# Branch mixture with the branch outermost, and seven of its column pairs by block products

## The chip, the cores and the metric

One core of a Trainium2 chip runs the whole program in one launch. The metric is device microseconds of one execution. The times before the change are 2878.73, 2878.84 and 2879.1 us; the median is 2878.84 us.

## The reference, cut to what matters

Four layers run on a sequence of 512 rows with 1024 columns in float32: two hybrid layers, then a pooling layer and an attention layer. The change is in the two hybrid layers, at the end of their first half:

```python
branches = jnp.stack([ret, gla_o, fox_o], axis=2).astype(h.dtype)
y_br = jnp.einsum('bsnw,nwd->bsnd', branches, w_br)
gates = jax.nn.sigmoid(h @ w_mg + b_mg).reshape(b, s, N_BRANCH, D_MODEL)
mixed = jnp.sum(gates * y_br, axis=2) @ w_o
x = x + (gate1[:, None, :] * mixed).astype(x.dtype)
h2 = modulate(rms_norm(x, norm2_g), shift2, scale2)
u, g = jnp.split(h2 @ w_up, 2, axis=-1)
```

Three branches of 512 columns each are projected to 1024 columns, weighted by three gates of 1024 columns that come from the normed input `h`, summed, and projected by `w_o`. A feed-forward part with 2816 columns (22 tiles of 128) follows.

## The kernel before

**Products.** Every float32 factor is kept as a high part (fp32r) and a low remainder, and a product is three matmuls: high by high, high by low, low by high (`dot`, L490 to L504; the matmuls are L496 to L498). A *tile* is 128 output columns by 512 rows: eight input blocks by three matmuls, 24 matmuls of 512 columns, summed in one PSUM bank (`tile_of`, L509). A weight *chunk* (128 by 1024 numbers, 512 KB) is loaded by SyncE's queue into one of six slots (L3391); ScalarE writes its high part (L1503, four chunks ahead) and GpSimd its low part in place of the raw numbers (L3376). A slot is loaded again once TensorE has done with its chunk.

**Banks.** `take_bank` (L484) hands out PSUM banks in turn from the list that is in force, and one running count serves all lists: `b = self.order[self.turn % len(self.order)]`. The lists are BIG3 (b0, b1, b2), BIG4 (b0, b1, b2, o) and BIG6 (b0, b1, b2, o, s0, s1). The count is set to 0 at the end of the prologue (L737) and at the start of the attention layer (L1324), and nowhere between. TensorE waits, before the first matmul into a bank, for the event that `free` holds for it: the instruction that last read the bank's previous contents. A *take* is one such call.

**Order of the work in a hybrid layer** (`schedule`, L400): retention, forgetting attention, gated linear attention, `gated` (eight tiles), the mixture, `w_o`, the feed-forward part `ffn`, `w_down`. Each engine has its own written-out program in the same order and runs it strictly in that order; semaphores tie them together. In the first hybrid layer, the chunks of `ada` (modulation weights, worked on by VectorE at L2526, with a short folding product at L782 that takes a bank) are stepped beside the mixture and later work.

**The mixture** (`mixing`: TensorE L1099, ScalarE L1916, VectorE L2815). A *unit* is one branch and one pair of output tiles `d` = 2dp, 2dp+1. TensorE makes two gate tiles (`mg`, 24 matmuls each) and two branch tiles (`br`, four blocks by three, 12 matmuls each) and takes four banks. ScalarE puts the sigmoid of a gate tile in SG (L1927); VectorE multiplies the branch tile with it (L2829 or L2832) and adds to the sum MX (L2834). After the third branch, ScalarE writes the high part MH (L1934) and VectorE the low part ML (L2838) of the finished tile. The 12 units of a layer run with dp outside and the branches 0, 2, 1 inside; MX has room for two tiles. Two units run beside `gla_attention`, under BIG3; then come the four tiles of `gated(l, 1)` under BIG3, and ten units under BIG4. `w_o` (`out_proj`, L1137) starts with three output tiles at once, block by block (L1164 to L1166), so that it takes three banks within its first nine matmuls. It stays under BIG4.

**The feed-forward part** (`ffn`: TensorE L1197, ScalarE L2052, VectorE L3018). Tiles `up` and `gateup` alternate, f = 0 to 21. The first four f (HEAD, eight takes) stand under BIG4, then BIG6 holds to the end of `ffn`, and `w_down` is under BIG4 again. The bank of `up` f is free when VectorE's second convolution step has read it (`conv`, L2895; a layer of the first two has `up_freed` = `conv`); that of `gateup` f when VectorE has multiplied it (L2903). For some f (`PAIRS_OF`) the two tiles are made together by `pair` (L1232) in the manner of Strassen and Winograd: seven half products of 4 blocks by 3 matmuls of 256 columns (84 matmuls, L1226 to L1228), in place of 48 matmuls of 512 columns; it takes three banks in place of two. Its operands are sums: of quarters of the input (TR, TH, TL: once per layer, `halves_whole` L2919, `halves_sums` L2927, `halves_low` L2939 on VectorE, `halves_high` L2007 on ScalarE), and of quarters of the two weight chunks (ER, EH, EL and one chunk slot: `pair_sums` L2947, `pair_low` L2965, `pair_high` L2014). The parts of the result that two quarters share go through MP (`pair_copies` L2030, `pair_out` L2984). The sums of the input are made by VectorE during f = 1 to 3, between the convolutions.

Of the kernel before, what the change touches and what calls it, by code (L numbers as in the profile page):

```python
# [64 lines left out]
def pair_block(i, f):  # L65

    return PAIRS_OF[i].index(f) % 2
# [187 lines left out]
class Kernel:  # L255
# [26 lines left out]
    def block(self, i, f):  # L282

        b = pair_block(i, f)
        return tuple(self.t[x][:, b, :, :] for x in ("EH", "EL", "ER"))
# [17 lines left out]
def ffn_norm(i):  # L303
    return (1, 3, 5, 7)[i]
# [160 lines left out]
class TensorSteps(Steps):  # L465
# [633 lines left out]
    def mixing(self, l, dp, branches):  # L1099
# [6 lines left out]
        for n in branches:  # L1106
            for u in range(2):
                d = 2 * dp + u
                key = ("mg", l, d, n)
                yield from self.project(wmg, n * 1024 + d * 128, key, lambda key=key: m.atake.at(*key))  # L1110
# [26 lines left out]
    def out_proj(self, name, i, norm):  # L1137
# [6 lines left out]
        place = (lambda k: (LAST + k) % ROOM) if name in ("w_down", "ffn_w_down") else (lambda k: k)  # L1144
# [52 lines left out]
    def ffn(self, i):  # L1197
# [10 lines left out]
        for f in range(HEAD, KF):  # L1208
            if f not in PAIRS_OF[i]:
                for key, ap, c0, freed in jobs(f):  # L1210
                    for _ in self.project(ap, c0, key, freed):
                        yield BUSY if f == KF - 1 else None
            else:
                yield from self.pair(i, f, up_freed)
            if f in DOWN:
                yield from self.down(i, wd, *DOWN[f])
# [15 lines left out]
    def pair(self, i, f, up_freed):  # L1232

        m, t, K = self.m, self.t, self.K
        wu, cu, wg, cg, _ = ffn_weights(self.I, i)
        na = self.weight(wu, 0, 8, cu + f * 128, 128)
        nb = self.weight(wg, 0, 8, cg + f * 128, 128)
# [9 lines left out]
        T1, T3, T2, T4 = [(t["TH"][:, j, :, :], t["TL"][:, j, :, :]) for j in range(4)]  # L1247
        left, right = slice(0, 256), slice(256, 512)

        def H(j, c):  # L1250
            return t["HH"][:, 4 * j:4 * j + 4, c], t["HL"][:, 4 * j:4 * j + 4, c]

        bc_, ba, bd = [self.take_bank((x, i, f)) for x in ("up", "mid", "gateup")]
# [9 lines left out]
                          [("up", i, f)])  # L1263
        yield BUSY
        self.half_product(G[:, left], A22, T4, True, [m.vtake.at("t", i, 3), m.atake.at("mid5", i, f)],
                          [("gateup", i, f), ("chunk", na), ("chunk", nb)])
        yield BUSY
        self.free[ba] = m.vtake.at("mid", i, f)
        self.free[bc_] = up_freed(f)
        self.free[bd] = m.vtake.at("gateup", i, f)  # L1270
# [215 lines left out]
class ScalarSteps(Steps):  # L1486
# [429 lines left out]
    def mixing(self, l, dp, branches):  # L1916
        e, q, m, t = self.e, self.q, self.m, self.t
        c = pcol(l, "b_mg")
        for n in branches:
            for u in range(2):  # L1920
                d = 2 * dp + u
                key = ("mg", l, d, n)
                yield from self.tile()
                j = c + 8 * n + d
                before = ("mixed", l, d, (None, 2, 0)[n]) if n else ("mixed", l, d - 2, 1)
                q.wait_ge(m.dense.at(*key), m.vtake.at(*before) if n or dp else None)
                e.activation(t["SG"][:, u, :], self.bank[self.K.where.get(key, "b0")][:, :], ACT.Sigmoid,  # L1927
                             bias=t["PAR"][:, j:j + 1]).then_inc(*m.atake.up(key))
            self.chunk()
            yield None  # L1930
            yield None
        for d in (2 * dp, 2 * dp + 1) if n == 1 else ():
            q.wait_ge(m.vtake.at("mixed", l, d, 1))
            e.activation(t["MH"][:, d, :], t["MX"][:, d % 2, :], ACT.Copy).then_inc(*m.atake.up(("mh", l, d)))  # L1934
# [95 lines left out]
    def pair_copies(self, i, f, late):  # L2030

        e, q, m, t, K = self.e, self.q, self.m, self.t, self.K
        A, G = [self.bank[K.where.get((x, i, f), "b0")] for x in ("mid", "gateup")]
# [3 lines left out]
        e.activation(t["MP"][:, 0:3:2, :], A[:, :].rearrange("p (h c) -> p h c", h=2), ACT.Copy,  # L2037
# [4 lines left out]
        e.activation(t["MP"][:, 1, :], G[:, 256:512], ACT.Copy).then_inc(*m.atake.up(("mid5", i, f)))  # L2042
# [240 lines left out]
class VectorSteps(Steps):  # L2283
# [531 lines left out]
    def mixing(self, l, dp, branches):  # L2815
        e, q, m, t = self.e, self.q, self.m, self.t
        SG, MX = t["SG"], t["MX"]
        for n in branches:
            for u in range(2):
                yield from self.tile()  # L2820
            self.next_chunk()
            for u in range(2):
                d = 2 * dp + u
                yield None
                out = self.out_of(("br", l, d, n))
                q.wait_ge(m.dense.at("br", l, d, n), m.atake.at("mg", l, d, n))
                if n == 0:
                    q.wait_ge(m.vtake.at("mix", l, d - 2) if dp else None)
                    e.tensor_tensor(MX[:, u, :], out[:, :], SG[:, u, :], ALU.mult).then_inc(  # L2829
                        *m.vtake.up(("br", l, d, 0), ("mixed", l, d, 0)))  # L2830
                else:
                    e.tensor_tensor(SG[:, u, :], out[:, :], SG[:, u, :], ALU.mult).then_inc(*m.vtake.up(("br", l, d, n)))  # L2832
                    q.wait_ge(m.vtake.at("br", l, d, n))
                    e.tensor_tensor(MX[:, u, :], MX[:, u, :], SG[:, u, :], ALU.add).then_inc(  # L2834
                        *m.vtake.up(("mixed", l, d, n)))
# [83 lines left out]
    def halves_whole(self, i):  # L2919

        e, q, m, t = self.e, self.q, self.m, self.t
        for j, (k, c) in enumerate(((0, 0), (0, 256), (4, 256), (4, 0))):
            q.wait_ge(m.vnorm.at("h", ffn_norm(i), 1, 7))
            e.tensor_tensor(t["TR"][:, j, :, :], t["HH"][:, k:k + 4, c:c + 256].bitcast(F32),
                            t["HL"][:, k:k + 4, c:c + 256].bitcast(F32), ALU.add).then_inc(*m.vtake.up(("whole", i, j)))

    def halves_sums(self, i):  # L2927

        e, q, m, TR = self.e, self.q, self.m, self.t["TR"]
        q.wait_ge(m.vtake.at("whole", i, 1))  # L2930
        e.tensor_tensor(TR[:, 0, :, :], TR[:, 1, :, :], TR[:, 0, :, :], ALU.subtract).then_inc(*m.vtake.up(("traw", i, 0)))
        q.wait_ge(m.vtake.at("whole", i, 2), m.vtake.at("traw", i, 0))
        e.tensor_tensor(TR[:, 1, :, :], TR[:, 2, :, :], TR[:, 1, :, :], ALU.subtract).then_inc(*m.vtake.up(("traw", i, 1)))
        q.wait_ge(m.vtake.at("traw", i, 1))
        e.tensor_tensor(TR[:, 2, :, :], TR[:, 0, :, :], TR[:, 2, :, :], ALU.subtract).then_inc(*m.vtake.up(("traw", i, 2)))
        q.wait_ge(m.vtake.at("whole", i, 3), m.vtake.at("traw", i, 2))
        e.tensor_tensor(TR[:, 3, :, :], TR[:, 3, :, :], TR[:, 2, :, :], ALU.add).then_inc(*m.vtake.up(("traw", i, 3)))

    def halves_low(self, i, js):  # L2939

        e, q, m, t = self.e, self.q, self.m, self.t
        for j in js:
            q.wait_ge(m.atake.at("t", i, j))
            e.tensor_tensor(t["TL"][:, j, :, :], t["TR"][:, j, :, :], t["TH"][:, j, :, :].bitcast(F32),
                            ALU.subtract).then_inc(*m.vtake.up(("t", i, j)))

    def pair_sums(self, i, f):  # L2947
# [8 lines left out]
        before = pair_before(i, f, 2)  # L2956
# [27 lines left out]
    def pair_out(self, i, f, row):  # L2984

        e, q, m, t = self.e, self.q, self.m, self.t
        A, MP = self.out_of(("mid", i, f)), t["MP"]
        if row == 0:
            q.wait_ge(m.dense.at("up", i, f), m.atake.at("mid", i, f), m.atake.at("mid5", i, f))
# [4 lines left out]
            C = self.out_of(("up", i, f))[:, :].rearrange("p (h c) -> p h c", h=2)  # L2994
            e.tensor_tensor(C, C, MP[:, 0:2, :], ALU.subtract).then_inc(*m.vtake.up(("out1", i, f)))
        else:
            q.wait_ge(m.dense.at("gateup", i, f), m.vtake.at("mid", i, f))
            G = self.out_of(("gateup", i, f))[:, :].rearrange("p (h c) -> p h c", h=2)
# [454 lines left out]
def places(nc):  # L3453
    with ExitStack() as ctx:
# [199 lines left out]
```

## Time and profile before

| | us |
|---|---|
| median of three runs | 2878.84 |
| the profiled execution | 2875.43 |
| its span, first to last instruction | 2873.6 |
| TensorE busy | 2838.0 (99% of the span) |
| VectorE busy | 1606.0 (56%) |
| ScalarE busy | 1176.6 (41%) |
| GpSimd busy | 1123.3 (39%) |
| mean granted TensorE clock (share of 2.4 GHz) | 0.998 |

The profiled execution is 1.8 us longer than its span. It is one execution; the three timed runs lie within 0.4 us of each other and their median is 3.4 us above it. Times in the rows are counted from the first instruction. Matmuls are pipelined: the duration of one in a row is longer than the distance to the start of the next, and that distance is what a stream of matmuls costs.

### The profile page before, as it was taken

What the parts mean: (1) busy time and instruction counts of PE and PEld (TensorE: products, weight loads), DVE (VectorE), ACT (ScalarE), POOL (GpSimd) and SP (SyncE); (2) the same over time, 40 slices, a digit from 0 to 9 for tenths busy, and PEclk for the clock granted to TensorE, in tenths of its full rate; (3) what the DMA queues carried; (4) which work ended last, traced back from release to release, by engine and by line L of the source; (5) the groups of instructions that cost most, each with busy time, mean ns of one, the idle gap of its engine ahead of it and who ended that gap; (6) DMA issues with size and microseconds to landing.
All of it is one profiled execution on the core that took longest, in us unless ns stands there. A gap on an engine that the chain in (4) does not pass through costs nothing.

```text
span 2873.6 us, 37367 instructions
## 1 busy us (share of the span) xinstructions
PE 2838.0 (99%) x15599; PEld 2397.8 (83%) x15599; DVE 1606.0 (56%) x2244; ACT 1176.6 (41%) x1797; POOL 1123.3 (39%) x461
## 2 busy tenths in 40 slices
PE   8999999999999999999999999999999999999999
PEld 5777888888888877788898988888999877789998
DVE  6444572367675624422266755648668456676683
ACT  4336333342333424532344434444334466443433
POOL 2332345334445332344435344543334423333432
PEclk9999999999999999999999999999999999999999
DMA  8331353346564422233333333333333322233332
GB/s 259 104 103 52 100 194 117 95 141 202 195 200 127 113 80 59 74 96 96 88 101 92 97 107 89 103 96 92 100 110 103 104 67 67 75 93 98 109 103 76
DMA packets 507292, 314.25 MB, mean 109 GB/s; under 512 B 14290, under 2 KB 478836, under 8 KB 506868
## 3 DMA queue, kind: packets, MB, share of 16 engines
q1 hardware_dynamic: 507124, 311.87, 37.0%
q8 instruction: 123, 2.02, 0.3%
q14 instruction: 45, 0.37, 0.0%
HBM read 309.73 MB, written 2.10 MB: 109 GB/s over the span
## 4 chain that ended last, share of the span: by engine, by line
PE 93%; DVE 3%; ACT 1%; DMA 1%; SPq 1%; issue 0%; POOL 0%; DVEq 0%; ACTq 0%
PE b L496 16%; PE b L498 16%; PE b L497 16%; PE o L496 4%; PE o L498 4%; PE o L497 4%; PE s L498 3%; PE s L496 3%; PE s L497 3%; PE b L1226 2%; PE b L1228 2%; PE b L1227 2%; PE s L1226 1%; PE s L1228 1%; PE s L1227 1%; PE b L1164 1%
## 5 line engine op out<-in xcount | busy, mean ns | idle before, releaser
L3376 POOL TENSOR_TENSOR lo<-raw,hi 128x1024 fp32r<-128x1024 f32 (+2 forms) x451 | 1121.0, 2496 | 1721.1 <-ACT hi L1503 1371.8
L1503 ACT ACTIVATE hi<-raw 128x1024 fp32r<-128x1024 f32 (+2 forms) x454 | 464.5, 1035 | 318.7 <-DMA raw<-in_w_up_dram 92.9
L496 PE MATMUL b<-HH,hi 128*128 128x512 f32 x1296 | 517.7, 399 | 0.0
L498 PE MATMUL b<-HH,lo 128*128 128x512 f32 x1296 | 505.2, 390 | 0.0
L497 PE MATMUL b<-HL,hi 128*128 128x512 f32 x1296 | 505.1, 390 | 0.0
L496 PEld LDWEIGHTS b<-HH,hi 128*128 128x128 f32 x1296 | 243.3, 188 | 57.9 <-issue 7.1
L498 PEld LDWEIGHTS b<-HH,lo 128*128 128x128 f32 x1296 | 243.3, 188 | 51.9
L497 PEld LDWEIGHTS b<-HL,hi 128*128 128x128 f32 x1296 | 243.5, 188 | 50.2 <-issue 1.4
L2526 DVE SCALAR_TENSOR_TENSOR AA<-raw,CA,AA 128x512 f32<-128x512 f32 x140 | 143.5, 1025 | 3.5
L496 PE MATMUL b<-FH,hi 128*128 128x512 f32 (+1 forms) x385 | 141.7, 368 | 0.9 <-POOL lo L3376 0.9
L497 PE MATMUL b<-FL,hi 128*128 128x512 f32 (+1 forms) x385 | 141.3, 367 | 0.0
L498 PE MATMUL b<-FH,lo 128*128 128x512 f32 (+1 forms) x385 | 141.3, 367 | 0.0
L2909 DVE TENSOR_TENSOR FL<-CB,FH 128x512 fp32r<-128x512 f32 x88 | 82.6, 938 | 62.2 <-ACT FH L1997 62.2
L2021 ACT ACTIVATE EH<-ER 128x1024 fp32r<-128x1024 f32 x38 | 40.3, 1062 | 179.3 <-DVE ER L2958 179.3
L1997 ACT ACTIVATE FH<-CB 128x512 fp32r<-128x512 f32 x88 | 55.6, 632 | 126.6 <-DVE CB L2903 125.6
L1990 ACT ACTIVATE CB<-CB 128x512 f32<-128x512 f32 x88 | 55.4, 630 | 121.6 <-DVE CB L2895 72.0
L2832 DVE TENSOR_TENSOR SG<-b,SG 128x512 f32<-128x512 f32 x21 | 14.5, 691 | 155.6 <-PE b L498 155.6
L496 PE MATMUL o<-HH,hi 128*128 128x512 f32 x248 | 96.5, 389 | 0.0
L497 PE MATMUL o<-HL,hi 128*128 128x512 f32 x248 | 96.5, 389 | 0.0
L498 PE MATMUL o<-HH,lo 128*128 128x512 f32 x248 | 96.5, 389 | 0.0
L1927 ACT ACTIVATE SG<-b,PAR 128x512 f32<-128x512 f32 x43 | 29.6, 689 | 155.3 <-PE b L498 155.3
L2977 DVE TENSOR_TENSOR lo<-raw,hi 128x1024 fp32r<-128x1024 f32 x38 | 90.0, 2369 | 0.0
(654 smaller groups left out, 6837.9 us busy)
## 6 DMA issues: line engine op xcount, KB each, us to landing
raw<-in_w_up_dram SPq DMA_DIRECT2D x88, 512.0 KB, 4.1
raw<-in_w_ada_dram SPq DMA_DIRECT2D x80, 512.0 KB, 4.9
raw<-in_w_in_dram SPq DMA_DIRECT2D x76, 512.0 KB, 4.1
raw<-in_w_mg_dram SPq DMA_DIRECT2D x48, 512.0 KB, 3.8
raw<-in_ffn_w_gate_dram SPq DMA_DIRECT2D x44, 512.0 KB, 3.9
raw<-in_ffn_w_up_dram SPq DMA_DIRECT2D x44, 512.0 KB, 3.9
raw<-in_w_down_dram SPq DMA_DIRECT2D x32, 448.0 KB, 3.8
raw<-in_ffn_w_down_dram SPq DMA_DIRECT2D x32, 448.0 KB, 3.9
```

The costliest lines, as they stand in the source:

```text
L496: e.matmul(out, wh, xh, start=start and k == 0, stop=False)
L497: e.matmul(out, wh, xl, start=False, stop=False)
L498: mm = e.matmul(out, wl, xh, start=False, stop=stop and k == last)
L1226: e.matmul(out, wh[:, c], xh[:, k, :], start=start and k == 0, stop=False, skip_group_check=True)
L1227: e.matmul(out, wh[:, c], xl[:, k, :], start=False, stop=False, skip_group_check=True)
L1228: mm = e.matmul(out, wl[:, c], xh[:, k, :], start=False, stop=k == 3, skip_group_check=True)
L1503: e.activation(t["hi"][:, c % NSLOT, 0:w], K.raw[:, c % NSLOT, 0:w], ACT.Copy).then_inc(*m.hi.up(c))
L1997: e.activation(t["FH"][:, f % ROOM, :], t["CB"][:, f % 2, :], ACT.Copy).then_inc(*m.atake.up(("fh", i, f)))
L2526: a = e.scalar_tensor_tensor(out=AA[:, :], in0=raw[:, k * 512:k * 512 + 512], scalar=CA[:, kk:kk + 1], in1=AA[:, :], op0=ALU.mult, op1=ALU ...
L2909: e.tensor_tensor(t["FL"][:, f % ROOM, :], t["CB"][:, f % 2, :], t["FH"][:, f % ROOM, :].bitcast(F32), ALU.subtract).then_inc(*m.vtake.up( ...
L2977: e.tensor_tensor(t["lo"][:, s, :], K.raw[:, s, :], t["hi"][:, s, :].bitcast(F32), ALU.subtract).then_inc(*m.vtake.up(("lo", na + 1 if K.p ...
L3376: e.tensor_tensor(t["lo"][:, s, 0:w], K.raw[:, s, 0:w], t["hi"][:, s, 0:w].bitcast(F32), ALU.subtract).then_inc(*m.lo.up(n))
```

## The change

The mixture is turned around in both layers: the branch is the outer loop (0, 2, 1) and dp the inner one, as units f = 0 to 11. The sum MX has eight tiles and stays raw until the third branch; MH and ML are then written in the last four units, ML in place of MX. Units 2 to 11 run under BIG6 in place of BIG4. In the second hybrid layer alone, units 5 to 11 make their two gate tiles by `pair`, with one buffer of weight sums in place of two, and with the pair's shared parts (mMP) in the place of SG. The sums of the input for it are made in units 2 to 4. `ffn` and the rest keep their lists and their code; `out_proj` reads MH and ML at shifted places. The core of the diff:

```diff
-            (5, 6, 7, 8, 9, 10, 12, 13, 14, 15, 16, 17, 19, 20))
+            (5, 6, 7, 8, 9, 10, 12, 13, 14, 15, 16, 17, 19, 20),
+            (), (5, 6, 7, 8, 9, 10, 11))
+MIX_BRANCHES = (0, 2, 1)
...
-    return PAIRS_OF[i].index(f) % 2
+    return PAIRS_OF[i].index(f) % 2 if i < 4 else 0
...
-        fill = chain(P.gated(l, 0), P.mixing(l, 0, (0, 2)))
+        fill = chain(P.gated(l, 0), P.mixing(l, (0, 1)))
         weave(P.gla_attention(l), fill)
         drain(beside(P.gated(l, 1), ada, 8))
+        P.order = BIG6
+        drain(beside(P.mixing(l, range(2, 12)), ada, 28))
         P.order = BIG4
-        drain(beside(chain(P.mixing(l, 0, (1,)), *[P.mixing(l, dp, (0, 2, 1)) for dp in (1, 2, 3)]), ada, 28))
...
+        for f in units:
+            n, dp = MIX_BRANCHES[f // 4], f % 4
+            keys = [("mg", l, 2 * dp + u, n) for u in range(2)]
+            if f in PAIRS_OF[4 + l]:
+                c0 = n * 1024 + dp * 256
+                yield from self.pair(4 + l, f, (wmg, c0), (wmg, c0 + 128), m.atake.at(*keys[0]), m.atake.at(*keys[1]))
...
-        bc_, ba, bd = [self.take_bank((x, i, f)) for x in ("up", "mid", "gateup")]
+        bc_, ba, bd = [self.take_bank(key) for key in (up, ("mid", i, f), gate)]
...
+                q.wait_ge(m.vtake.at("out%d" % (u + 1), i, f) if pair else m.dense.at(*key),
+                          m.vtake.at("mixed", l, 2 * ((f - 1) % 4) + u, MIX_BRANCHES[(f - 1) // 4]) if f else None)
...
+            if f == 3 and PAIRS_OF[i]:
+                self.halves_high(i, (0, 1, 2))
+            if f == 4 and PAIRS_OF[i]:
+                q.wait_ge(m.dense.at("br", l, 7, 0))
+                self.halves_high(i, (3,))
...
+        if i >= 4:
+            q.wait_ge(m.vtake.at("mixed", i - 4, 2 * ((f - 1) % 4) + 1, MIX_BRANCHES[(f - 1) // 4]))
...
+            if f == 2 and PAIRS_OF[i]:
+                self.halves_whole(i)
+            if f == 3 and PAIRS_OF[i]:
+                self.halves_sums(i)
...
+            if f in PAIRS_OF[i]:
+                self.next_chunk()
+                self.next_chunk()
+                yield BUSY
+                yield BUSY
+                if g is not None:
+                    self.pair_sums(i, g)
+                yield BUSY
+                self.pair_out(i, f, 0)
+                yield BUSY
+                self.pair_out(i, f, 1)
+                if g is not None:
+                    self.pair_low(i, g, 0)
...
+            self.next_chunk()
+            yield None
+            branch(0)
+            if g is not None:
+                self.pair_low(i, g, 1)
+            yield None
+            branch(1)
+            if g is not None:
+                self.pair_low(i, g, 2)
...
-        before = pair_before(i, f, 2)
+        before = pair_before(i, f, 2 if i < 4 else 1)
         q.wait_ge(m.dense.at("block", i, before) if before is not None else None)
...
-        area("MH", 36, [128, 8, S], F32R)
+        area("MH", 28, [128, 8, S], F32R)
         area("ML", 20, [128, 8, S], F32R)
+        area("MX", 20, [128, 8, S])
         area("SG", 8, [128, 2, S])
-        area("MX", 10, [128, 2, S])
+        area("mMP", 8, [128, 3, 256])
```

Here g is the next unit where that one is made by `pair`, and `branch(u)` is the multiplication and the addition of one branch tile.

## Rows read from the trace of the kernel before

**Rows 1.** The page: busy time, share of the span and instructions by engine.

```profile
PE 2838.0 (99%) x15599; PEld 2397.8 (83%) x15599; DVE 1606.0 (56%) x2244; ACT 1176.6 (41%) x1797; POOL 1123.3 (39%) x461
```

**Rows 2.** Windows, both mixtures: length, busy per engine, clock, DMA share, GB/s.

```profile
300.00:545.00 245.00, 245.00 (x1192) 201.87 (x1191) 114.49 (x133) 82.20 (x99) 104.80 (x43) 1.00 0.42 130
1250.00:1425.60 175.60, 175.60 (x776) 145.46 (x775) 37.13 (x44) 54.13 (x66) 78.35 (x33) 1.00 0.33 96
```

**Rows 3.** Timeline of TensorE in layer 2's mixture: two matmuls, 36 apart.

```profile
1384.81 0.39 PE L496 MATMUL b<-HH,hi 128*128 128x512 f32 x1
...
1392.97 0.39 PE L496 MATMUL b<-HH,hi 128*128 128x512 f32 x1
```

**Rows 4.** Timeline of TensorE: a pair's first matmul, the first after its 84.

```profile
2697.94 0.28 PE L1226 MATMUL s<-HH,hi 128*128 128x256 f32 x1
...
2708.02 0.40 PE L496 MATMUL b<-FH,hi 128*128 128x512 f32 x1
```

**Rows 5.** By source line: the pair's work on VectorE; ns shortest/median/longest.

```profile
L2958 DVE TENSOR_TENSOR ER<-raw x38: 1212/1216/1220, 1542.0 to 2789.8; 128x1024 f32<-128x1024 f32 x38
L2981 DVE TENSOR_TENSOR EL<-ER,EH x38: 677/683/2891, 1549.3 to 2797.1; 128x512 fp32r<-128x512 f32 x38
L2977 DVE TENSOR_TENSOR lo<-raw,hi x38: 1209/2338/3444, 1546.0 to 2793.8; 128x1024 fp32r<-128x1024 f32 x38
L2995 DVE TENSOR_TENSOR b<-b,MP x19: 698/699/700, 1617.2 to 2806.9; 128x512 f32<-128x512 f32 x19
L2834 DVE TENSOR_TENSOR MX<-MX,SG x32: 692/1212/1999, 338.4 to 1426.5; 128x512 f32<-128x512 f32 x32
```

**Rows 6.** Timeline of VectorE at the head of layer 2's feed-forward part.

```profile
1495.64 9.03 DVE L2924 TENSOR_TENSOR TR<-HH,HL 128x1024 f32<-128x1024 f32 x4
...
1515.83 2.55 DVE L2944 TENSOR_TENSOR TL<-TR,TH 128x1024 fp32r<-128x1024 f32 x2
...
1521.12 4.55 DVE L2944 TENSOR_TENSOR TL<-TR,TH 128x1024 fp32r<-128x1024 f32 x2
1525.59 0.74 DVE L2892 SCALAR_TENSOR_TENSOR CB<-b,PAR,CB 128x511 f32<-128x511 f32 x1
1526.36 0.75 DVE L2895 SCALAR_TENSOR_TENSOR CB<-b,PAR,CB 128x510 f32<-128x510 f32 x1
1527.87 0.69 DVE L2903 TENSOR_TENSOR CB<-CB,b 128x512 f32<-128x512 f32 x1 [0.77 <-PE b L498]
```

**Rows 7.** Timeline of TensorE there: the first matmul of `up` 4.

```profile
1516.77 0.39 PE L496 MATMUL s<-HH,hi 128*128 128x512 f32 x1
```

**Rows 8.** Timeline of ScalarE there: the activation after the convolution of f = 3.

```profile
1527.14 0.63 ACT L1990 ACTIVATE CB<-CB 128x512 f32<-128x512 f32 x1 [5.89 <-DVE CB L2895]
```

**Rows 9.** Windows at the kernel's start; the granted clock is the third number from the end.

```profile
15.00:20.00 5.00, 2.03 (x10) 2.03 (x10) 3.85 (x6) 4.41 (x7) 0.00 (x0) 0.66 1.13 327
20.00:25.00 5.00, 5.00 (x24) 2.21 (x23) 2.73 (x4) 1.21 (x2) 0.00 (x0) 0.50 1.10 348
25.00:30.00 5.00, 4.12 (x30) 1.29 (x28) 3.58 (x7) 1.38 (x2) 0.00 (x0) 0.82 1.10 348
```

**Rows 10.** Timeline of TensorE there: after an idle stretch, and twice the same work.

```profile
17.97 0.59 PE L722 MATMUL t<-ones,SS 128*128 128x1 f32 x2 [3.45 <-DVE SS L2375]
...
21.48 4.13 PE L697 MATMUL s<-ada,CA 128*32 128x512 f32 x16
...
35.42 2.34 PE L697 MATMUL s<-ada,CA 128*32 128x512 f32 x16
```

**Rows 11.** Timelines: the last tile ahead of `w_o`, and of `w_down`, and their readers.

```profile
1425.61 0.39 PE L1164 MATMUL b<-MH,hi 128*128 128x512 f32 x1
...
1425.81 0.69 DVE L2832 TENSOR_TENSOR SG<-o,SG 128x512 f32<-128x512 f32 x1 [0.78 <-PE o L498]
...
1782.97 0.39 PE L1164 MATMUL b<-FH,hi 128*128 128x512 f32 x1
...
1783.17 0.69 DVE L2903 TENSOR_TENSOR CB<-CB,b 128x512 f32<-128x512 f32 x1 [3.09 <-PE b L498]
```

More of the change, by code:

```diff
@@ L303, in ffn_norm @@
 def ffn_norm(i):
-    return (1, 3, 5, 7)[i]
+    return (1, 3, 5, 7, 0, 2)[i]
 def norm_weights(t, nid):
@@ L1143, in out_proj @@
         halves = WHOLE[nid]
-        place = (lambda k: (LAST + k) % ROOM) if name in ("w_down", "ffn_w_down") else (lambda k: k)
+        place = ((lambda k: (LAST + k) % ROOM) if name in ("w_down", "ffn_w_down") else
+                 (lambda k: (k + 4) % 8) if name == "w_o" else (lambda k: k))
         def entries(d):
@@ L1213, in ffn @@
             else:
-                yield from self.pair(i, f, up_freed)
+                yield from self.pair(i, f, (wu, cu + f * 128), (wg, cg + f * 128), up_freed(f), m.vtake.at("gateup", i, f))
             if f in DOWN:
@@ L1230, in half_product, with pair @@
             mm.then_inc(*m.dense.up(*keys))
-    def pair(self, i, f, up_freed):
+    def pair(self, i, f, above, below, up_freed, gate_freed):
         m, t, K = self.m, self.t, self.K
-        wu, cu, wg, cg, _ = ffn_weights(self.I, i)
-        na = self.weight(wu, 0, 8, cu + f * 128, 128)
-        nb = self.weight(wg, 0, 8, cg + f * 128, 128)
+        up, gate = pair_keys(i, f)
+        na = self.weight(above[0], 0, 8, above[1], 128)
+        nb = self.weight(below[0], 0, 8, below[1], 128)
         assert nb == na + 1
@@ L2032, in pair_copies @@
         e, q, m, t, K = self.e, self.q, self.m, self.t, self.K
-        A, G = [self.bank[K.where.get((x, i, f), "b0")] for x in ("mid", "gateup")]
+        A, G = [self.bank[K.where.get(key, "b0")] for key in (("mid", i, f), pair_keys(i, f)[1])]
+        MP = t["MP" if i < 4 else "mMP"]
         g = pair_before(i, f, 1)
@@ L2813, in gated, with mixing, branch @@
                 *m.vtake.up(("gated", l, which, h)))
-    def mixing(self, l, dp, branches):
+    def mixing(self, l, units):
         e, q, m, t = self.e, self.q, self.m, self.t
         SG, MX = t["SG"], t["MX"]
[L2818 to L2822, printed above, removed]
+        i = 4 + l
+        for f in units:
+            n, dp = MIX_BRANCHES[f // 4], f % 4
+            g = f + 1 if f + 1 in PAIRS_OF[i] else None
+            def branch(u):
                 d = 2 * dp + u
-                yield None
+                p = (d + 4) % 8
                 out = self.out_of(("br", l, d, n))
@@ new lines, in mixing @@
+            if f == 3 and PAIRS_OF[i]:
+                self.halves_sums(i)
+            if f == 4 and PAIRS_OF[i]:
+                q.wait_ge(m.dense.at("br", l, 7, 0))
+            if f in PAIRS_OF[i]:
+                self.next_chunk()
+                self.next_chunk()
+                yield BUSY
+                yield BUSY
+                if g is not None:
+                    self.pair_sums(i, g)
+                yield BUSY
+                self.pair_out(i, f, 0)
+                yield BUSY
+                self.pair_out(i, f, 1)
+                if g is not None:
+                    self.pair_low(i, g, 0)
+            else:
+                if g is not None:
+                    self.pair_sums(i, g)
+                for _ in self.tile():
+                    yield BUSY if f == 4 else None
+                if g is not None:
+                    self.pair_low(i, g, 0)
+                for _ in self.tile():
+                    yield BUSY if f == 4 else None
+                if f == 3 and PAIRS_OF[i]:
+                    self.halves_low(i, (0, 1, 2))
+                if f == 4 and PAIRS_OF[i]:
+                    self.halves_low(i, (3,))
@@ new lines, in mixing @@
+            self.next_chunk()
+            yield None
+            branch(0)
+            if g is not None:
+                self.pair_low(i, g, 1)
+            yield None
+            branch(1)
+            if g is not None:
+                self.pair_low(i, g, 2)
+            for d in (2 * dp, 2 * dp + 1) if n == 1 else ():
+                q.wait_ge(m.atake.at("mh", l, d))
+                p = (d + 4) % 8
+                e.tensor_tensor(t["ML"][:, p, :], MX[:, p, :], t["MH"][:, p, :].bitcast(F32), ALU.subtract).then_inc(
+                    *m.vtake.up(("mix", l, d)))
@@ L2986, in pair_out @@
         e, q, m, t = self.e, self.q, self.m, self.t
-        A, MP = self.out_of(("mid", i, f)), t["MP"]
+        up, gate = pair_keys(i, f)
+        A, MP = self.out_of(("mid", i, f)), t["MP" if i < 4 else "mMP"]
         if row == 0:
-            q.wait_ge(m.dense.at("up", i, f), m.atake.at("mid", i, f), m.atake.at("mid5", i, f))
+            q.wait_ge(m.dense.at(*up), m.atake.at("mid", i, f), m.atake.at("mid5", i, f))
             e.tensor_tensor(MP[:, 1:3, :], MP[:, 1:3, :],
```

123 lines of the change are left out of this document (77 added, 46 removed).

## The prediction

> **What bounds the kernel now.** I read the page first: TensorE is busy for 99% of the span [rows 1], so only what TensorE issues, and the time in which it issues nothing, can count. Then the windows over the two mixtures: TensorE is busy in every microsecond of both, at full clock, while VectorE works 37 of 176 us in layer 2's and 114 of 245 us in layer 1's [rows 2]. There is no stall in the mixture to be removed. A gain can only come from fewer or shorter matmuls, and a loss from a wait that the new order puts in front of TensorE. Then the timelines for the price of a matmul, and last, because the change alters how many banks are taken, the places where the list of banks changes.
>
> **What is removed and added on TensorE.** In a stream, 36 matmuls of 512 columns take 1392.97 - 1384.81 = 8.16 us, 0.2267 us each [rows 3]; the 84 matmuls of a pair take 2708.02 - 2697.94 = 10.08 us, 0.120 us each [rows 4]. Two gate tiles cost 48 x 0.2267 = 10.88 us, a pair 10.08 us: 0.80 us less. Seven pairs in one layer: **-5.60 us**. The branch tiles stay, so a pair unit lasts 10.08 + 24 x 0.2267 = 15.52 us. The Trainium skill (TensorE: Matmul & The Clock Gate, Back-to-back issue gap) prices a warm matmul at N / 2.4 GHz plus 2.5 ns, about 109 ns at 256 columns and 216 ns at 512; by that the pairs would give 8.3 us. The rows say 120 and 227 ns, and I take the rows.
>
> **Can the pairs be fed?** The buffer of weight sums is single now, so VectorE starts the next unit's sums only when five of the seven half products are done: 60 x 0.120 + 0.28 = 7.5 us after the pair's start. From there, in VectorE's order: sums of 1024, 512 and 512 numbers, 1.22 + 0.69 + 0.69, done at 10.2; three combining steps of 0.7, 12.2; the low part of the first sums, as wide as L2958, 1.22; branch tile 0 (a multiplication of 0.69 and an addition of 0.69 to 2.0); a low part of 1.2 to 3.4; branch tile 1, for whose product it must wait to 15.7; the last low part, 0.68 [rows 5]. The long ends are those of operations that meet a low part on GpSimd: L2977 lasts 3.44 at most against 1.21, so 2.2 are lost to one such meeting [rows 5]. GpSimd makes two low parts per unit; with one meeting of 0.4 and one of 2.0 the chain ends at about 20.5. TensorE wants the last one for the fifth half product of the next pair, at 15.52 + 5.76 = 21.3. So it holds with 0.8 us to spare: cost **0**, upper end 1 us in each of six pairs. ScalarE's new wait for the previous unit's sum before it writes mMP (it lies over SG) ends at 19.8; TensorE needs that copy at 22.7. Behind it stand only the highs of the unit after. GpSimd's and SyncE's queues keep three chunks per unit in the same order; two slots now come free together, at 10.1 us, and the next use is 15 us on. The sums of the input (12 operations of 1.2 us, up to 3.4) fall into units 2 to 4, where VectorE was idle for four fifths of the time [rows 2]; they delay ScalarE's highs by some 7 us, and those run four chunks, some 20 us, ahead. The reordered sums, MH, ML and the folds are the same operations at other times; they cost nothing while VectorE has that room, and if it had not, branch banks would come free late, which six banks allow for 10 us.
>
> **The bank count.** This is where I expect the time to go. The count is never reset in the hybrid layers, so I count takes from the zero at L737. Layer 1 up to `w_o`: 8 + 4 + 16 + 6 + 4 + 8 + 4 + 40 and two folds = 92, before and after. The rest of layer 1 (11 + 60 + 11, four folds) gives 178; layer 2 up to `w_o` gives 268 before. Now each pair takes one bank more: 275. `w_o` takes 11, so `ffn` begins at 279 before and 286 after. Before, `up` 4 is take 287, and 287 mod 6 = 5 is s1: the row of `up` 4 indeed shows an s bank [rows 7]. After, `up` 3 is take 292, under BIG4 that is b0; `up` 4 is take 294, under BIG6 also **b0**. The bank that came round after several takes comes round after two.
>
> `up` 4 must therefore wait for the convolution of f = 3. VectorE ends that at 1526.36 + 0.75 = 1527.11 [rows 6], because the sums of the input stand in front of it: 9.03 us for the first four, then ScalarE's part, then 2.55 and 4.55 us for the low parts [rows 6]. None of that waits for `up` 4. TensorE could start `up` 4 at 1516.77 [rows 7]. A semaphore passes to ScalarE in 0.03 us [rows 8]; with 0.2 us for TensorE to pick up weights and start, the wait is 1527.11 - 1516.77 + 0.2 = **+10.5 us**. Behind it on TensorE stands everything; ScalarE and VectorE catch up meanwhile. `gateup` 4 then sits in gate 3's bank, read at 1527.87 + 0.69, long before TensorE gets there. Bounds: if the second group of low parts went as quickly as the first, 2.55 in place of 4.55, the wait is 8.5 us; if the first group were as slow as the second, 12.5.
>
> **The clock after the wait.** At the start of the kernel TensorE was idle for 3.45 us [rows 10], and the granted clock averages 0.66 in that window, 0.50 in the next, 0.82 in the third [rows 9]: it fell to 1.2 GHz at about 16.6 us, still idle, and rose to 2.4 GHz at about 26.8 us, 5.3 us after the dense work at 21.48 began. The same 16 matmuls took 4.13 us at the lower level and 2.34 at the higher [rows 10]. An idle time of 10.5 us should do the same. 5.3 us of work at 2.34/4.13 of the speed gives away 5.3 x (1 - 0.567) = **+2.3 us**; bounds 0 and 4.
>
> **Two small waits of the same kind.** Under BIG6 the last two branch tiles of layer 1 are takes 90 and 91, b0 and b1; `w_o`'s first three are 92 to 94 under BIG4: b0, b1, b2. The second wants the last branch tile's bank 3 x 0.2267 = 0.68 us after `w_o`'s start. Before, that tile's reader starts 0.20 us after `w_o`'s first matmul and lasts 0.69 [rows 11]: free at 0.89, a wait of some 0.2, with the restart **+0.4 us** (0 to 1). Layer 2's `w_o` gets o, b0, b1, whose readers are long done. At the end of layer 2's `ffn` (62 takes under BIG6: ten pairs, eight plain f, 16 for `down`) the count is 356 in place of 349: `w_down` starts on b0, b1, b2 and the last `gateup` tile is take 355, b1. Its reader also starts at 0.20 and lasts 0.69 [rows 11]: **+0.4 us**. From there lists of four follow lists of four until the third layer's head, which gets a distance of four; the attention layer sets the count to zero.
>
> **The sum.** -5.6 + 10.5 + 2.3 + 0.4 + 0.4 = +8.0 us. Against the profiled execution's own 2875.43 us that is 2883.4. That execution is 3.4 us under the median of the timed runs, so as a median I predict 2878.84 + 8.0 = **2886.8 us**. The case's own range is 2882 to 2891: the wait's bounds (2 either way) and the clock's, not all at once.
>
> **The rivals.**
> 1. *No wait at `up` 4.* If the bank is not the same one, or its reader is done by then, what is left is -5.6 + 0.4 + 0.4 = -4.8: **2874.0 us**, not slower. For it: the old kernel starts `up` 4 without a stall. Against: the count reproduces the s bank before, and VectorE's 1527.11 does not depend on TensorE. It decides if VectorE's convolution of f = 3 ends by 1516.8, 10.3 us earlier than now.
> 2. *A shorter wait and no fall of the clock.* 8.5 us and 0: -5.6 + 8.5 + 0.8 = +3.7, **2882.5 us**, inside 0.2%. For it: the second low parts were slowed by GpSimd, which may stand otherwise. Against: ScalarE's and GpSimd's order there is untouched.
> 3. *The pairs stall too.* Single buffer, VectorE in its long durations at every step: six more pairs at 1 us and the forecast's terms: +14, **2892.8 us**. For it: 3.44 and 2.89 us stand in the rows for low parts [rows 5]. Against: a unit has only two GpSimd operations to run into.
> 4. *The pairs gain by the formula.* 8.3 us in place of 5.6 by a matmul stream that runs at the pure column rate: +5.3, 2884.1 us. Every pair in the trace runs at 0.120. That is the rule of the skill's page above.
>
> **How the numbers follow.** Chances: the forecast 0.72, rival 1 0.11, rival 2 0.09, rival 3 0.07, rival 4 0.01. 0.2% of the time is 5.8 us, about what a measurement of this kernel can tell from no change. The forecast lies over it, as does rival 3: slower 0.80 with a little of rival 2's upper end. Rival 1 at -4.8 lies within it, unless its small terms vanish and something more is won: 0.03 faster, 0.08 same. With rivals 2 and 4 the same is 0.17. The range must leave out no more than 0.2: it takes in the forecast's own, rival 2, part of rival 3, and the 3 us by which single executions differ: 2878 to 2892.
>
> **What would show it.** In the changed trace: pairs in layer 2's mixture of 84 starts 0.120 us apart and no gap between units; at the head of layer 2's `ffn` one idle stretch of TensorE of some 10 us ahead of `up` 4, ended by VectorE's L2895, `up` 4 in a b bank, and a clock of 0.50 for some 5 us behind it; gaps under 0.5 us in `w_o` of layer 1 and `w_down` of layer 2. No such stretch there makes the prediction wrong at its main step; gaps ahead of the fifth half product would speak for rival 3.

## The result and the profile after

The changed kernel takes 2887.69 us (median of 7 runs, 2884.65 to 2888.86), the kernel before, measured again beside it, 2877.94 (median of six): a ratio of **1.0034**, 95% interval 1.0025 to 1.0044. A seventh run of the kernel before took 3338.28 us, far off all others, and is left out (with it the median is 2878.73). The changed kernel is slower by more than the 0.2% that can be told, and 0.9 us above the predicted 2886.8. The profiled execution took 2886.1 us with a span of 2884.3, 10.7 more than the span before.

The page after, which answers to [rows 1]:

```profile
PE 2836.4 (98%) x15851; PEld 2406.2 (83%) x15851; DVE 1682.8 (58%) x2319; ACT 1198.8 (42%) x1829; POOL 1111.5 (39%) x454
```

The 252 matmuls more are seven pairs (84 for 48 each). TensorE is busy 1.6 us less although the span is 10.7 longer: it waits. The waits view of TensorE from 1240 to 1530 us shows on whom (us in total, times, longest):

```profile
PE b L514 <- DVE CB L3000: 10.2, 1, 10.2
PE b L1251 <- DVE mEL L3087: 0.7, 1, 0.7
```

L3000 is the second convolution step (L2895 before). The timelines of TensorE and of VectorE there, which answer to [rows 6] and [rows 7]:

```profile
1512.79 0.39 PE L516 MATMUL b<-HH,lo 128*128 128x512 f32 x1
1523.40 0.77 PE L514 MATMUL b<-HH,hi 128*128 128x512 f32 x1 [10.22 <-DVE CB L3000]
1523.96 0.63 PE L515 MATMUL b<-HL,hi 128*128 128x512 f32 x1
```

```profile
1517.32 4.49 DVE L3051 TENSOR_TENSOR TL<-TR,TH 128x1024 fp32r<-128x1024 f32 x2
1521.73 0.74 DVE L2997 SCALAR_TENSOR_TENSOR CB<-b,PAR,CB 128x511 f32<-128x511 f32 x1
1522.50 0.75 DVE L3000 SCALAR_TENSOR_TENSOR CB<-b,PAR,CB 128x510 f32<-128x510 f32 x1
```

TensorE has finished gate 3 and stands ahead of `up` 4, now in a b bank, until VectorE has convolved f = 3: 1523.40 - 1512.79 less the 0.227 of a matmul, 10.38 us lost. The convolution stands behind the low parts of the input's sums, exactly as before.

The windows show the clock (third number from the end): the mixture, the wait, the 5 us behind it, and 5 us at the start of the attention layer's output product:

```profile
1280.00:1425.00 145.00, 144.31 (x913) 131.36 (x912) 112.62 (x113) 64.69 (x85) 51.63 (x20) 1.00 0.35 102
1512.00:1523.40 11.40, 1.18 (x7) 0.67 (x5) 10.52 (x9) 3.94 (x6) 6.08 (x3) 0.70 0.16 46
1523.40:1528.40 5.00, 5.00 (x15) 4.03 (x16) 3.15 (x2) 2.93 (x4) 3.46 (x2) 0.66 0.00 0
2477.80:2482.80 5.00, 4.93 (x15) 3.89 (x16) 4.83 (x7) 1.75 (x4) 0.00 (x0) 0.66 0.00 0
```

Behind the wait the clock is at 1.2 GHz at first; the distances of the matmuls there add up to 1.7 us over 0.2267 each. The last row is a second stretch of that kind, of 1.6 us, in a stage that nobody touched. The kernel before has the same 5 us of work at full clock:

```profile
2468.80:2473.80 5.00, 4.97 (x22) 4.13 (x23) 4.84 (x6) 1.80 (x4) 0.00 (x0) 1.00 0.01 3
```

The pairs (TensorE's timeline: the first matmul of the first pair, the first behind its 84, the first of the next pair) take 10.08 us and a unit 15.54:

```profile
1312.08 0.28 PE L1251 MATMUL b<-HH,hi 128*128 128x256 f32 x1
...
1322.16 0.40 PE L514 MATMUL o<-EfH,hi 128*128 128x512 f32 x1
...
1327.62 0.28 PE L1251 MATMUL s<-HH,hi 128*128 128x256 f32 x1
```

Six of the seven are like that. The seventh waits ahead of its fifth half product (TensorE, then VectorE and GpSimd):

```profile
1410.96 0.28 PE L1253 MATMUL b<-mTH,mEL 128*128 128x256 f32 x1
1411.92 0.39 PE L1251 MATMUL b<-HH,mEH 128*128 128x256 f32 x1 [0.69 <-DVE mEL L3087]
```

```profile
1404.23 2.37 DVE L2896 TENSOR_TENSOR MX<-MX,SG 128x512 f32<-128x512 f32 x1
1406.52 3.42 DVE L3083 TENSOR_TENSOR lo<-raw,hi 128x1024 fp32r<-128x1024 f32 x1
...
1411.19 0.68 DVE L3087 TENSOR_TENSOR mEL<-mER,mEH 128x512 fp32r<-128x512 f32 x1
```

```profile
1403.64 5.22 POOL L3483 TENSOR_TENSOR lo<-raw,hi 128x1024 fp32r<-128x1024 f32 x2 [1.12 <-ACT hi L1528]
```

VectorE's addition takes 2.37 us in place of 0.69 and its low part 3.42 in place of 1.21 [rows 5] while GpSimd makes two low parts in a row. The Trainium skill (SBUF — State Buffer, Who interferes with whom) says that a VectorE instruction with two inputs in SBUF contends with a GpSimd instruction that reads SBUF, and that this contention is an exclusive lock; the low part's row, which ends 1.1 us after GpSimd's two (1403.64 + 5.22 = 1408.86), agrees.

The two small waits, in `w_o` of layer 1 and `w_down` of layer 2 (TensorE; the matmul ahead of each started 0.58 us earlier, so 0.35 us is lost in each):

```profile
527.46 0.47 PE L1189 MATMUL b<-MH,hi 128*128 128x512 f32 x1 [0.20 <-DVE SG L2894]
...
1792.36 0.47 PE L1189 MATMUL b<-FH,hi 128*128 128x512 f32 x1 [0.19 <-DVE CB L3008]
```

The balance against the span before: -5.6 (pairs) + 10.4 + 1.7 + 0.7 (two small waits) + 1.0 (last pair, with its restart) + 1.6 (second low stretch) = 9.8 of the 10.7 us. The rest came in pieces under 0.3 us over the program, 0.4 us of it ahead of anything that was changed, and was not located further.

### The profile page after: what moved, and what is told of

Same layout as the page of the kernel before. It is cut to its first block, busy times and chain, and to the rows that moved or that the text cites. A ratio compares the mean times of both kernels' runs of the same rounds, so it can differ in the third digit from the quotient of the medians.

```text
span 2884.3 us, 37975 instructions
## 1 busy us (share of the span) xinstructions
PE 2836.4 (98%) x15851; PEld 2406.2 (83%) x15851; DVE 1682.8 (58%) x2319; ACT 1198.8 (42%) x1829; POOL 1111.5 (39%) x454
## 4 chain that ended last, share of the span: by engine, by line
PE 91%; DVE 5%; ACT 2%; DMA 1%; SPq 1%; issue 1%; POOL 0%; DVEq 0%; ACTq 0%
PE b L514 14%; PE b L516 14%; PE b L515 14%; PE s L514 4%; PE s L516 4%; PE s L515 4%; PE o L514 3%; PE o L516 3%; PE o L515 3%; PE b L1251 3%; PE b L1253 3%; PE b L1252 3%; PE s L1251 2%; PE s L1253 1%; PE s L1252 1%; PE b L1189 1%
## 5 line engine op out<-in xcount | busy, mean ns | idle before, releaser
L3483 POOL TENSOR_TENSOR lo<-raw,hi 128x1024 fp32r<-128x1024 f32 (+3 forms) x444 | 1109.2, 2508 | 1743.6 <-ACT hi L1528 1314.2
L1528 ACT ACTIVATE hi<-raw 128x1024 fp32r<-128x1024 f32 (+1 forms) x447 | 457.0, 1034 | 312.9 <-DMA raw<-in_w_up_dram 92.8
L514 PE MATMUL b<-HH,hi 128*128 128x512 f32 x1136 | 456.4, 402 | 10.2 <-DVE CB L3000 10.2
L515 PE MATMUL b<-HL,hi 128*128 128x512 f32 x1136 | 443.5, 390 | 0.0
L516 PE MATMUL b<-HH,lo 128*128 128x512 f32 x1136 | 443.5, 390 | 0.0
L514 PEld LDWEIGHTS b<-HH,hi 128*128 128x128 f32 x1136 | 213.7, 188 | 62.3 <-issue 17.7
L516 PEld LDWEIGHTS b<-HH,lo 128*128 128x128 f32 x1136 | 213.7, 188 | 46.0
L2587 DVE SCALAR_TENSOR_TENSOR AA<-raw,CA,AA 128x512 f32<-128x512 f32 x140 | 145.5, 1040 | 3.3
L514 PE MATMUL s<-HH,hi 128*128 128x512 f32 x272 | 105.9, 389 | 0.0
L515 PE MATMUL s<-HL,hi 128*128 128x512 f32 x272 | 105.9, 389 | 0.0
L516 PE MATMUL s<-HH,lo 128*128 128x512 f32 x272 | 105.8, 389 | 0.0
```

The lines of the kernel that those rows point to most:

```text
L514: e.matmul(out, wh, xh, start=start and k == 0, stop=False)
L515: e.matmul(out, wh, xl, start=False, stop=False)
L516: mm = e.matmul(out, wl, xh, start=False, stop=stop and k == last)
L1528: e.activation(t["hi"][:, c % NSLOT, 0:w], K.raw[:, c % NSLOT, 0:w], ACT.Copy).then_inc(*m.hi.up(c))
L2587: a = e.scalar_tensor_tensor(out=AA[:, :], in0=raw[:, k * 512:k * 512 + 512], scalar=CA[:, kk:kk + 1], in1=AA[:, :], op0=ALU.mult, op1=ALU ...
L3483: e.tensor_tensor(t["lo"][:, s, 0:w], K.raw[:, s, 0:w], t["hi"][:, s, 0:w].bitcast(F32), ALU.subtract).then_inc(*m.lo.up(n))
```

## The experiments

Two rivals were set against the theory of the bank count: that the turned mixture itself makes VectorE late, whatever the bank (B), and that a shorter wait leaves the clock alone (C). All times below are against the kernel before in the same session; its medians lay between 2876.1 and 2877.3 us.

**1. The count alone set back.** The changed kernel, with

```diff
+        if l == 1:
+            P.turn = 268
         P.mods(l, 1)
         drain(P.out_proj("w_o", l, P.x_norm(2 * l + 1)))
```

> The changed kernel, with the bank count of layer 2 set back to 268 ahead of w_o, where the old kernel has it; the matmuls, the pairs and all other orders are the changed kernel's. Theory A (the loss is the bank that comes round after two takes): the idle stretch of 10.2 us ahead of up 4 is gone, and with it the 1.7 us at 1.2 GHz behind it and the 0.35 us in w_down of layer 2; left are seven pairs (-5.66), the one stall of 1.0 us in the last pair and 0.36 us in w_o of layer 1, so -4.3 us against the kernel before, a ratio of 0.9985 (0.997 to 1.000). Rival B (VectorE, made late by the turned mixture, holds TensorE up at the head of the feed-forward part whatever the bank): the idle stretch stays within 2 us of 10, and the ratio stays at 1.003.

Measured: 2871.92 us (11 runs), ratio **0.9981** (0.9972 to 0.9990). The timelines of TensorE, the last matmul of gate 3 and the first of `up` 4, and of VectorE:

```profile
1513.72 0.39 PE L518 MATMUL b<-HH,lo 128*128 128x512 f32 x1
1513.94 0.39 PE L516 MATMUL s<-HH,hi 128*128 128x512 f32 x1
```

```profile
1522.78 0.74 DVE L2999 SCALAR_TENSOR_TENSOR CB<-b,PAR,CB 128x511 f32<-128x511 f32 x1
1523.55 0.75 DVE L3002 SCALAR_TENSOR_TENSOR CB<-b,PAR,CB 128x510 f32<-128x510 f32 x1
```

VectorE ends the convolution of f = 3 at 1523.55 + 0.75 = 1524.30. Counted from the first matmul of `w_o` (1422.79 here, 1425.61 before, 1421.86 after) that is 101.5 us, as before (101.5) and after (101.4). TensorE, in an s bank again, has been in `up` 4 for 10.4 us by then. The lateness is the same; only the bank made it a wait. Rival B falls. The stall of the last pair is still there, 0.73 us. (The profiled execution, span 2870.8, began slowly: the first 297 us took 1.4 us more than before, ahead of anything that was changed.)

**2. The count alone set on.** The kernel before, with its own mixture, and `P.turn = 275` at the same place.

> The kernel before, with its old mixture and no pairs in it, and the bank count of layer 2 set on by seven, to 275, ahead of w_o. Theory A: the idle stretch of 10 us ahead of up 4 appears here too, up 4 in a b bank, a clock of 0.50 for some 4 us behind it and 0.35 us more in w_down of layer 2: +12.4 us, a ratio of 1.0043 (1.003 to 1.006). Rival B (the turned mixture is what makes VectorE late): no idle stretch and a ratio of 1.000.

Measured: 2890.26 us (5 runs), ratio **1.0045** (1.0033 to 1.0058). TensorE's timeline, at `w_o` and at `up` 4, and the window behind it:

```profile
1426.57 0.47 PE L1166 MATMUL o<-MH,hi 128*128 128x512 f32 x1 [0.88 <-DVE SG L2834]
...
1528.18 0.77 PE L498 MATMUL b<-HH,hi 128*128 128x512 f32 x1 [10.21 <-DVE CB L2897]
```

```profile
1528.18:1533.18 5.00, 5.00 (x13) 3.95 (x14) 3.14 (x2) 2.93 (x4) 3.46 (x2) 0.56 0.00 0
```

One number, set from 268 to 275 in a kernel that is otherwise untouched, costs 10.4 us at `up` 4, 2.2 in the clock behind it, 0.35 in `w_down`, and 1.0 in `w_o`, which I had missed: under the old BIG4 the last branch tile (take 267) sits in o, and take 275 is o again.

**3. Turned around, no pairs.** `PAIRS_OF[5] = ()` in the changed kernel.

> The changed kernel with the mixture turned around in both layers but no pairs in layer 2's: 48 matmuls of 512 columns per unit as before, and the count at its old place by itself. Theory A: turning the mixture around costs nothing but the 0.36 us in w_o of layer 1; no idle stretch ahead of up 4, no small one in w_down of layer 2: +0.4 us, a ratio of 1.0001 (0.999 to 1.001). Rival B: the idle stretch of 10 us stays, +12 us, a ratio of 1.004.

Measured: 2878.33 us (11 runs), ratio 1.0003 (0.9994 to 1.0012). TensorE at the head of the feed-forward part:

```profile
1500.00:1530.00 30.00, 30.00 (x134) 24.86 (x133) 24.14 (x20) 13.01 (x16) 12.99 (x6) 1.00 0.32 93
```

No wait in 30 us, full clock. Turning the loops costs nothing that can be measured.

**4. A shorter wait.** The changed kernel; the second group of low parts goes behind the convolution of f = 3.

```diff
-                if j in (4, 5):
-                    self.halves_low(i, (2 * j - 8, 2 * j - 7))
+                if j in (4, 6):
+                    self.halves_low(i, (j - 4, j - 3))
```

> The changed kernel, count and bank collision left as they are, but VectorE makes the second group of low parts of the input's sums (4.5 us) behind its convolution of f = 3 instead of ahead of it. Theory A: the convolution ends 4.5 us earlier and so does the wait: an idle stretch of 5.9 us in place of 10.4, still ended by the second convolution step; the clock still falls behind it, for at most as long (up to 1.7 us): -4.5 us against the changed kernel, +4.2 us against the kernel before, a ratio of 1.0015 (1.000 to 1.003). Rival C (the clock doesn't fall for the shorter idle): 1.7 us less, +2.5 us, ratio 1.0009. Rival B: the idle stretch keeps its length.

Measured: 2881.65 us (11 runs), ratio 1.0017 (1.0008 to 1.0025). TensorE at `up` 4, VectorE's convolution, and two windows of 5 us behind the wait:

```profile
1518.66 0.76 PE L514 MATMUL b<-HH,hi 128*128 128x512 f32 x1 [6.04 <-DVE CB L3000]
```

```profile
1517.76 0.75 DVE L3000 SCALAR_TENSOR_TENSOR CB<-b,PAR,CB 128x510 f32<-128x510 f32 x1
```

```profile
1518.66:1523.66 5.00, 5.00 (x12) 3.94 (x13) 4.30 (x4) 3.04 (x4) 3.80 (x3) 0.50 0.00 0
1523.66:1528.66 5.00, 5.00 (x23) 4.10 (x22) 1.22 (x3) 0.78 (x1) 2.65 (x1) 0.95 0.07 18
```

The wait follows VectorE's order: 6.2 us lost in place of 10.4. Rival C falls, and so does "at most as long": behind the shorter wait the clock costs 2.7 us, more than the 1.7 behind the longer one. The profiled execution has two more low stretches in the attention layer, so its span stands high for its kernel.

**5. The last pair's stall.** The kernel of experiment 1, with

```diff
-            branch(1)
             if g is not None:
                 self.pair_low(i, g, 2)
+            branch(1)
```

> The kernel with the count set back, and in a pair unit VectorE makes the last low part of the next unit's sums ahead of the second branch tile instead of behind it. Theory A (the stall of 0.73 to 0.85 us in the last pair is the low part standing behind two operations that GpSimd slowed): the last low part comes at least 1.3 us earlier, no stall ahead of a fifth half product is left, the branch banks are read 0.7 us later and nobody waits for that: -5.3 us against the kernel before, a ratio of 0.9982 (0.997 to 0.999), 0.8 us under the kernel with the count set back, which only the trace can show. Rival D: the low part meets GpSimd at its new place as well and a stall over 0.5 us stays in some pair.

Measured: 2874.16 us (11 runs), ratio 0.9991 (0.9982 to 0.9999). A miss: the stall didn't go, it moved to the sixth half product and grew, from 0.73 us of waiting to 1.34 (TensorE, then ScalarE):

```profile
1414.20 0.39 PE L1253 MATMUL b<-mTH,hi 128*128 128x256 f32 x1 [1.34 <-ACT mMP L2100]
```

```profile
1413.57 0.58 ACT L2100 ACTIVATE mMP<-b 128x512 f32<-128x512 f32 x1
```

ScalarE may write mMP over the gates only when VectorE has added the previous unit's second tile, and that addition now comes later; a weight chunk's high part went in between. Both ends of VectorE's chain are wanted by TensorE; whichever stands last is late.

**6. Pairs in layer 1 too.** Experiment 5, with `PAIRS_OF[4] = (5, ..., 11)` and the count set to 92 and 268.

> The same, with seven pairs in layer 1's mixture as well and the bank count set to 92 and 268 ahead of the two w_o. Theory A (a pair saves 0.81 us of TensorE wherever it can be fed, and no bank comes round early): another -5.7 us, so -11 us against the kernel before, a ratio of 0.9962 (0.995 to 0.998), as long as VectorE, which steps the modulation chunks beside this mixture (102 us busy of 220 there), keeps up: some 8.5 us more per pair for it, 60 us in 110, so stalls up to 2 us per pair are possible. Rival E (VectorE becomes the bound in layer 1's mixture): stalls over 1 us ahead of the second or fifth half product in most pairs of layer 1, the gain there eaten, a ratio of 0.998 to 1.001.

Measured: 2880.88 us (11 runs), ratio 1.0013 (1.0004 to 1.0022). The largest wait of TensorE in that mixture, and the operation of VectorE that it stood behind:

```profile
PE s L801 <- DVE AS L2615: 5.5, 1, 5.5
```

```profile
366.43 6.83 DVE L3030 TENSOR_TENSOR mTR<-HH,HL 128x1024 f32<-128x1024 f32 x4
```

The fold of the modulation chunk waits for VectorE, which makes the sums of the input first. The clock falls in this wait, and the slow matmuls behind it cost another 2.7 us. VectorE is too full, as rival E has it, but the price stands mostly at one place: in the pairs of layer 1 four of seven wait, 0.1 to 0.9 us at a time. The ratio lies above both stated ranges.

**7. The operation that meets GpSimd goes last.** The kernel of experiment 1, with

```diff
             branch(0)
-            if g is not None:
-                self.pair_low(i, g, 1)
             yield None
             branch(1)
             if g is not None:
                 self.pair_low(i, g, 2)
+                self.pair_low(i, g, 1)
```

> The kernel with the count set back, and in a pair unit VectorE does both branch tiles first, then the last low part of the next unit's sums, then the low part that stands in the chunk slot. Theory A (VectorE's chain of a unit is too long by about 1 us in the one unit where two of its operations meet GpSimd, and both ends of it are wanted: the low part by the fifth half product, the finished sum by ScalarE, which writes the pair's shared part over the gates only then): with the operation that meets GpSimd moved to the end of the chain, where GpSimd has done, both ends come in time, no stall is left in the mixture, -5.3 us against the kernel before, a ratio of 0.9981 (0.997 to 0.999). Rival D: the low part in the slot is now too late for the sixth half product (wanted 7.2 us after the pair's start), a stall of 0.5 to 1.5 us there.

Measured: 2871.47 us (11 runs), ratio **0.9983** (0.9974 to 0.9992). VectorE's timeline ahead of the last pair:

```profile
1409.45 0.68 DVE L3088 TENSOR_TENSOR mEL<-mER,mEH 128x512 fp32r<-128x512 f32 x1
1410.05 1.22 DVE L3084 TENSOR_TENSOR lo<-raw,hi 128x1024 fp32r<-128x1024 f32 x1
```

The low part takes 1.22 us again, since GpSimd has done by then. An addition of a branch tile meets GpSimd in its place (2.18 us at 1407.35), and nobody waits for that. TensorE waits nowhere in the mixture. Against experiment 1 the 0.8 us cannot be told from none; the trace alone shows it.

**8 and 9. Layer 1 once more.** Experiment 7 with the pairs and counts of experiment 6; in 8 VectorE starts the sums of the input at the end of unit 2 instead of its beginning, in 9 ScalarE's highs and VectorE's lows of the sums also stand together in unit 4.

> The same with seven pairs in layer 1's mixture too, the bank count set to 92 and 268, and the sums of the input begun at the end of unit 2 instead of its start, so that the adds of the modulation chunk and its fold go first. Theory A: the stall of 5.6 us at the fold and the 2.6 us of low clock behind it are gone; the pairs of layer 1 save 5.7 us less 2 to 3.5 us of small stalls (GpSimd's and VectorE's low parts): -7.5 to -9 us against the kernel before, a ratio of 0.9971 (0.996 to 0.9985). Rival E: the fold waits for VectorE all the same, or the stalls of layer 1's pairs grow past 5 us: a ratio of 0.9985 or more.

> The kernel with seven pairs in both layers, with ScalarE's four high parts of the input's sums together at the start of unit 4, in both layers, and VectorE's four low parts at its end, so that ScalarE's highs of weight chunks no longer stand behind a wait for VectorE's sums in unit 3. Theory A (the 5.4 us stall in unit 3 of layer 1 is ScalarE's queue: its wait for the sums holds the high part of a chunk, GpSimd waits for that, TensorE for GpSimd): that stall and the low clock behind it are gone, small stalls of 2 to 3 us stay in layer 1: -7.5 to -9 us against the kernel before, a ratio of 0.9971 (0.996 to 0.9985). Rival E (VectorE simply has no room for the sums beside the modulation chunks): a stall of over 3 us comes at another place between units 3 and 5 of layer 1, and the ratio is 0.999 or more.

Measured: 8 2876.70 us, ratio 1.0001 (0.9992 to 1.0010); 9 2876.23 us, ratio 1.0000 (0.9991 to 1.0009), 11 runs each. Waits of TensorE in layer 1's mixture, in 8 and then in 9, with the operation of ScalarE behind each:

```profile
PE o L515 <- POOL lo L3483: 5.3, 1, 5.3
```

```profile
387.40 1.06 ACT L2071 ACTIVATE mTH<-mTR 128x1024 fp32r<-128x1024 f32 x1 [8.03 <-DVE mTR L3037]
```

```profile
PE b L515 <- POOL lo L3480: 3.7, 1, 3.7
PE o L1252 <- DVE mEL L3084: 2.6, 1, 2.6
```

```profile
400.62 1.06 ACT L1529 ACTIVATE hi<-raw 128x1024 fp32r<-128x1024 f32 x1 [11.85 <-DMA raw<-in_w_mg_dram]
```

In 8 ScalarE waits for VectorE's sums, and the high part of a weight chunk stands behind that wait; GpSimd and TensorE follow. In 9 ScalarE is free, and the next chunk comes late by its DMA. The waits of SyncE's queue in 9, from 384 to 400 us, say why:

```profile
SPq L3506 <- DVE AA L2587: 12.3, 1, 12.3
```

The chunk's slot held a modulation chunk, and VectorE (L2587) came to that one only behind the sums. The sums keep VectorE from the modulation chunks for 12 us in 8 (379.4 to 391.1) and 16 us in 9 (379.3 to 395.3), and the delay comes out at the next engine in line. The ratios are those of rival E both times. Its place is right in 9; in 8 the wait stands neither at the fold nor in a pair, but in unit 3.

## Why the prediction was right

- *The wait at `up` 4*: +10.5 predicted, 10.38 in the trace, in a b bank and ended by the convolution of f = 3. Experiments 1 and 2 take and give it with the count alone. The 0.2 us for TensorE's start came from no row; in the trace the first matmul starts 0.15 us behind the convolution (1523.40 against 1522.50 + 0.75 = 1523.25).
- *The pairs*: 10.08 us against 48 matmuls, -5.6 as forecast; rival 4 falls. The Trainium skill (TensorE: Matmul & The Clock Gate, Back-to-back issue gap) gives about 109 ns for a matmul of 256 columns by itself at 2.4 GHz; the pairs of the changed kernel do not show it, all seven run at 0.120 us per matmul outside the last one's wait. An estimate from the rows says why a pair saves no more: 256 columns more cost 0.2267 - 0.120 = 0.107 us, so 0.013 us of each matmul does not depend on its columns, and a pair has 36 matmuls more, some 0.5 us.
- *The feeding of the pairs*: "Cost 0, 0.8 us to spare, upper end 1 us in each of six pairs": five of these six cost nothing, the last cost 1.0. The step that failed is "one meeting of 0.4 and one of 2.0": ahead of the last pair VectorE met GpSimd twice at full length (2.37 for an addition of 0.69, 3.42 for a low part of 1.21). The chain ended 22.1 us after the sixth pair's start (1389.78 to 1411.87) in place of 20.5, and TensorE wanted it at 21.3, so rival 3 holds for that one pair.
- *The clock*: +2.3 predicted, from 5.3 us at the lower level; 1.7 in this trace, from 3.4 us; 2.2 and 2.7 in experiments 2 and 4, all inside the bounds of 0 and 4. That the fall comes was right; that an execution can be given one value was not.
- *The small waits*: 0.4 each predicted, 0.35 each measured.
- *Not in the sum*: 1.6 us of low clock in the attention layer.
- *Rivals 1 and 2*: rival 1 is what experiment 1 shows, once its condition is brought about by hand (its -4.8 us there measured as -5.4, 0.9981 of 2877.3); rival 2's shorter wait is experiment 4, and the clock falls all the same.

The sum of +8.0 us met +10.7 in the profiled executions and +9.8 between the medians (2887.69 against 2877.94). That the predicted 2886.8 lies only 0.9 us under the measured median is in part luck: it was added to the median of three runs, 2878.84, which is 0.9 us above that of the six. The executions of each kernel differ by 3 to 4 us among themselves, and the profiled one before was a quick one. The four slowest runs of the changed kernel have a mean clock of 0.994 or 0.995 against 0.996 in the profiled one; where they lost it no trace shows.

The change is worth having once the count is put right: experiments 1 and 7, at 0.9981 and 0.9983 with intervals that end under 1, beat the kernel before.

## What to carry to other kernels

When buffers are handed out by a running count, a change that takes one more of them moves every later stage onto other buffers, until the count is set again; count the takes up to each place where the list changes and look which late reader the next owner lands on. A late engine costs nothing as long as nobody comes back to its buffer: here the same lateness was free at a distance of several takes and cost 10 us at two. If an order beside the one bottleneck is full, moving an operation may only pick which engine is late next, as in experiments 5, 8 and 9; move the one that is slowed by its neighbour to where the neighbour is done (experiment 7).

## What the runs showed of the hardware

- **The clock's price did not grow with the idle time ahead of it.** Idle stretches of TensorE of 10.2, 10.2 and 6.0 us (the changed kernel, experiments 2 and 4) cost 1.7, 2.2 and 2.7 us of slow matmuls behind them, each at a distance of 0.43 us in place of 0.227. In experiments 6, 8 and 9 waits of 5.5, 5.3 and 3.7 us cost 2.7, 2.0 and 1.7. Each is one execution. By the windows shown the clock stayed at 1.2 GHz for some 3.4, 4.4 and 5.5 us behind the first three waits; what sets this length the runs don't show.
- **It also falls without a long idle.** In the changed kernel it was low for 3.4 us around 2480 us, where no idle time of TensorE in the 30 us before was over 1.9 us, and the kernel before, with the same work and the same idle times, kept 1.00 there in its profiled execution. The profiles of experiments 3 to 7 show such a stretch in the attention layer too, those of 1, 2, 8 and 9 don't. Those of 4 and 7 have another, at 2405 and 2396 us, with no idle time over 0.4 us in the 30 us before. The differences between executions go with the clock: of the 27 runs of the kernel before beside the first four experiments, all with a mean clock of 0.997 took 2877.6 us or more, and all under that had 0.998 or 0.999. What makes it fall in one execution and not in the next stays open.
